# Two late sums of squares made in halves of 128 columns

## The chip, the core and the metric

The kernel runs on one core of a Trainium2 chip. It is one launch that computes two transformer blocks, one after the other, for 256 positions of width 1024 in float32. The metric is the device time of that launch in microseconds (us), given as the median of several executions.

## The reference, cut to what matters

The second block normalises its input four times. Two of these norms, before the feed-forward part and before the last gate, are the ones that the change touches:

```python
def rmsnorm(x, g):
    y = xf * lax.rsqrt(jnp.mean(xf * xf, axis=-1, keepdims=True) + EPS)
    ...
h = rmsnorm(x, g_ffn[i])                    # tag "nff"
u = jnp.einsum("bsd,df->bsf", h, w_up[i])   # 1024 -> 5632
...                                         # conv, gelu, product with w_down
pg = jax.nn.sigmoid(jnp.einsum("bsd,de->bse", rmsnorm(x, g_ple[i]), w_ple_gate[i]))  # tag "np"
```

A norm needs, for each of the 256 positions, the sum of the squares over the 1024 channels.

## The kernel before, in words

**Layout.** Channels lie on the 128 partitions and positions on the free axis: `xT[:, k, :]` is the k-th group of 128 channels, 256 positions wide (`T` = 256, `P` = 128, `NT` = 2, `KD` = 8).

**Products.** Each float32 weight matrix is loaded in chunks by SyncE. ScalarE writes a rounded copy `w_hi` of each chunk (`part`, L1175), VectorE the remainder `w_lo` (`rest`, L1743), and the activations are split in the same way into `h_hi` and `h_lo`. One block of 128 output channels is made of 24 matmuls of 256 columns, three for each k: hi by hi (L673), lo by hi (L674), hi by lo (L675); see `three`. `product_parted` does one block after another. `abreast` does the first four blocks of a stage together, with k outermost, since the activations come one k at a time. In the product with `w_down` the three matmuls stand on L1100, L1101 and L1102.

**The late norms.** The factor of a norm is one number for each position, so it is applied after the product and not before. ScalarE squares `xT` into `sq`, VectorE adds the eight groups up into two (`gather_squares`), and TensorE makes the sum over the partitions with a matrix of ones: `sum_two` (L1077 to L1082). It is called inside `abreast`, after k = 6 in the stage `up` and after k = 4 in the stage `pg`. The result lies in bank 2 of PSUM; nothing else uses that bank then. ScalarE takes the root of it (`late_root`, L1201, one instruction over all 256 positions, which waits for the semaphore `norm_ss`), VectorE the reciprocal (`inverse`, L2197), and only then VectorE takes the first products out of their banks (`scaled`, L2250).

**Order.** Each engine has its own written order of work; semaphores link them. TensorE goes through `up` (11 chunks of four blocks, 44 blocks), `down` (8 chunks, 528 matmuls), `pg` (2 chunks) and the final transposes and sums (L1114, L1135) without a break in its program. `begin` (L636) makes a block wait for the chunk's `w_lo` and for its bank to be emptied. VectorE handles one chunk of `up` in a fixed order: two products scaled, a convolution with three taps, two products by the gelu, then `rest` (L1743) for the next chunk but one. SyncE loads a chunk when the last product of the third chunk before it is done (L510).

Of the kernel before, what the change touches and what calls it, by code (L numbers as in the profile page):

```python
# [21 lines left out]
P = 128  # L22
T = 256
NT = T // P
# [187 lines left out]
def two_blocks(nc, w, out):  # L212
    with ExitStack() as ctx:
        made = {}

        def S(name):

            if name not in made:
                made[name] = ctx.enter_context(nc.semaphore(name))
            return made[name]  # L220

        def sb(name, shape, dt=F32):
            return ctx.enter_context(nc.sbuf_tensor(name, shape, dt))

        ps = ctx.enter_context(nc.psum_tensor("ps", [P, 8, 512], F32))
        BK = [ps[:, b, :] for b in range(8)]
# [8 lines left out]
        ident, ones = sb("ident", [P, P]), sb("ones", [P, P])  # L235
# [6 lines left out]
        sq = sb("sq", [P, KD, T])  # L242
# [183 lines left out]
        def f_lo(b):  # L426
            return f_lo2[b // 16][:, b % 16, :]
# [205 lines left out]
        def _(pe):  # L633
# [121 lines left out]
            for i in range(2):  # L755
                mm = pe.matmul(BK[i], ones[0:1, :], c_all[0:1, i * 512:(i + 1) * 512], start=True, stop=True)
# [29 lines left out]
            for b in range(2):  # L786
# [3 lines left out]
                if b == 0:  # L790
                    pe.wait_ge(S("taken_A"), taken_by("A", BLOCK_AT[("low", 0)]))
                    for t in range(NT):
                        mm = pe.transpose(BK[7][:, t * IH:(t + 1) * IH], low[32:32 + IH, t * P:(t + 1) * P],
                                          ident[32:32 + IH, 32:32 + IH])
# [11 lines left out]
            for h in range(GH):  # L806
                mm = pe.matmul(BK[4 + h // 2][:, (h % 2) * T:(h % 2 + 1) * T], wgate[0:16, h * P:(h + 1) * P],
                               low[0:16, :], start=True, stop=True)
            mm.then_inc(S("gate_mm"), 1)
            for b in range(4):  # L810
                plain("gq", b)
                if b == 0:
                    pe.wait_ge(S("kv_h"), 1)
                    for t in range(NT):
                        for i in range(2):
                            mm = pe.transpose(BK[7][:, t * LAT + i * P:t * LAT + (i + 1) * P],
                                              kvT[:, i, t * P:(t + 1) * P], ident[:, :])
# [10 lines left out]
            for i in range(2):  # L828
                for j in range(4 * i, 4 * i + 4):
                    mm = pe.transpose(BK[6 + i][:, (j % 4) * P:(j % 4 + 1) * P], ediff[:, j * P:(j + 1) * P], ident[:, :])  # L830
                mm.then_inc(S("kend_mm"), 1)
                plain("gr", i)
            for i in range(2):
                pe.wait_ge(S("kendT"), i + 1)
                for j in range(4 * i, 4 * i + 4):
                    h, t = j // 2, j % 2
                    mm = pe.matmul(BK[6 + i][:, (j % 4) * P:(j % 4 + 1) * P], gk[:, h, t * P:(t + 1) * P],
                                   gq[:, h, t * P:(t + 1) * P], start=True, stop=True)
# [3 lines left out]
            for n in range(3):  # L842
                t, half = n // 2, slice((n % 2) * CH, (n % 2 + 1) * CH)
                if n:
                    pe.wait_ge(S("state"), n)
                for h in range(GH):
                    mm = pe.matmul(BK[6 + h // 2][:, (h % 2) * DV:(h % 2 + 1) * DV], kendT[half, 2 * h + t, :],
                                   gv[half, t, h * DV:(h + 1) * DV], start=True, stop=True)
# [4 lines left out]
            for h in range(GH):  # L853
# [4 lines left out]
                for b in range(2):  # L858
                    for t in range(NT):
                        o = BK[6 + h % 2][:, b * T + t * P:b * T + (t + 1) * P]  # L860
                        mm = pe.matmul(o, gv[:, t, h * DV + b * P:h * DV + (b + 1) * P], attn[:, 2 * h + t, :],
                                       start=True, stop=False, skip_group_check=True)
                        for n in (2 * t, 2 * t + 1):
                            if n:
                                c = (n % 2) * CH
                                mm = pe.matmul(o[:, c:c + CH], state[:, n - 1, h, b * P:(b + 1) * P],
                                               gq[:, h, t * P + c:t * P + c + CH], start=False, stop=n % 2 == 1,
                                               skip_group_check=True)
# [45 lines left out]
            for h in range(AH):  # L914
# [5 lines left out]
                if h == 0:  # L920

                    pe.wait_ge(S("o_sq"), GH)
                    for i in range(GH):
                        for b in range(2):
                            mm = pe.matmul(BK[6 + i // 2][:, (i % 2) * T:(i % 2 + 1) * T], ones[:, :], gT[:, 2 * i + b, :],
                                           start=b == 0, stop=b == 1)
# [108 lines left out]
            for k in range(KD):  # L1035
                mm = pe.matmul(BK[3][:, 0:T], g2e[:, k:k + 1].broadcast_to([P, P]), sq[:, k, :],
                               start=k == 0, stop=k == KD - 1)
            mm.then_inc(S("nm_ss"), 1)
            for b in range(4, 28):
                product_parted(("z", b), h_hi, h_lo)  # L1040
                if b == 11:

                    pe.wait_ge(S("nm_added"), 1)
                    for k in range(2):
                        mm = pe.matmul(BK[2][:, T:2 * T], ones[:, :], sq[:, k, :], start=k == 0, stop=k == 1)
                    mm.then_inc(S("nm_ss"), 1)
                if b == 19:
# [4 lines left out]
                    for i in range(2):  # L1052
                        for n in range(PE_TAPS):
                            tap = CK - PE_TAPS + n
                            mm = pe.matmul(BK[2 + i][:, 0:T], tap_diag[:, i * PE_TAPS + n, :],  # L1055
                                           apad[:, 2 + i, tap:tap + T], start=n == 0, stop=n == PE_TAPS - 1)
# [20 lines left out]
            def sum_two(tag):  # L1077

                pe.wait_ge(S(tag + "_added"), 1)
                for k in range(2):  # L1080
                    mm = pe.matmul(BK[2][:, 0:T], ones[:, :], sq[:, k, :], start=k == 0, stop=k == 1)
                mm.then_inc(S("norm_ss"), 1)  # L1082

            abreast("up", 4, h_hi, h_lo, "up", between=lambda: sum_two("nff"))
            for b in range(4, 2 * FB):
                product_parted(("up", b), h_hi, h_lo)
            for j in range(4):
                outs = [begin(("down", 2 * j + b))[0] for b in range(2)]
                for half in range(2):
# [3 lines left out]
                    for b in range(2):  # L1093
                        o, cs = outs[b][:, 0:T], slice(b * P, (b + 1) * P)
                        for k in range(FB // 2):
                            f = half * FB // 2 + k
                            if j == 0 and b == 0:
# [4 lines left out]
                            mm = pe.matmul(o, hi[:, k, cs], f_lo(f), start=False, stop=f == FB - 1,  # L1102
                                           skip_group_check=True)
# [6 lines left out]
            def turn_out(k):  # L1110
# [5 lines left out]
                mm.then_inc(S("out_mm"), 1)  # L1116

            abreast("pg", 4, h_hi, h_lo, "pg", between=lambda: sum_two("np"), after=4)
            for b in range(4, 8):
                product_parted(("pg", b), h_hi, h_lo)  # L1120
# [9 lines left out]
            for k in (0, 5, 6, 7):  # L1130
# [3 lines left out]
                for t in range(NT):  # L1134
                    mm = pe.matmul(BK[4 + t][:, 0:1], sq[:, k, t * P:(t + 1) * P], ones[:, 0:1],  # L1135
                                   start=k == 0, stop=k == KD - 1, skip_group_check=True)
# [1411 lines left out]
```

## Time and profile before

| what | value |
|---|---|
| time, median of 3 executions | 1404.92 us |
| the three executions | 1404.68, 1404.92, 1409.11 us |
| the profiled execution: span from its first to its last instruction | 1410.0 us |
| its time around the span | not given apart from the span |
| TensorE matmul busy | 1242.9 us (88%) |
| VectorE busy | 1070.5 us (76%) |
| ScalarE busy | 618.2 us (44%) |
| mean granted clock of TensorE | 0.977 |

The profiled execution is one execution of its own: its span alone is 5.1 us longer than the median of the three timed ones. Times in the trace are counted from the start of that span. TensorE's matmuls are pipelined: one begins about 0.11 us after the one before, while its record lasts 0.28 us, so durations overlap and the distance of starts is what counts.

### The profile page before, as it was taken

What the parts mean: (1) busy time and instruction counts of PE and PEld (TensorE: products, weight loads), DVE (VectorE), ACT (ScalarE), POOL (GpSimd) and SP (SyncE); (2) the same over time, 40 slices, a digit from 0 to 9 for tenths busy, and PEclk for the clock granted to TensorE, in tenths of its full rate; (3) what the DMA queues carried; (4) which work ended last, traced back from release to release, by engine and by line L of the source; (5) the groups of instructions that cost most, each with busy time, mean ns of one, the idle gap of its engine ahead of it and who ended that gap; (6) DMA issues with size and microseconds to landing.
All of it is one profiled execution on the core that took longest, in us unless ns stands there. A gap on an engine that the chain in (4) does not pass through costs nothing. (4 is left out here: it accounts for less than half of the span.)

```text
span 1410.0 us, 19695 instructions
## 1 busy us (share of the span) xinstructions
PE 1242.9 (88%) x7042; PEld 933.2 (66%) x7042; DVE 1070.5 (76%) x2161; ACT 618.2 (44%) x1268; POOL 286.6 (20%) x278
## 2 busy tenths in 40 slices
PE   4999999999989877777877877878899999999998
PEld 3999999999944332332322323323599989999998
DVE  6898568587879777776777777776599968998556
ACT  4566465546344332333333332233563245544445
POOL 1000000000445444444444444443000000000000
PEclk8999999999999999999999999999899999999999
DMA  9946534554989999999999999999743344444461
GB/s 393 381 153 239 209 111 188 176 183 150 370 340 426 428 427 427 427 428 427 427 427 427 427 428 427 428 427 427 314 178 136 143 180 180 180 180 161 169 228 42
DMA packets 55808, 416.65 MB, mean 295 GB/s; under 512 B 6049, under 2 KB 7713, under 8 KB 9394
## 3 DMA queue, kind: packets, MB, share of 16 engines
q0 software_dynamic: 36864, 268.45, 45.3%
q1 hardware_dynamic: 18544, 146.78, 28.1%
q8 instruction: 51, 0.84, 0.2%
q10 hardware_dynamic: 322, 0.36, 0.1%
q14 instruction: 27, 0.22, 0.0%
HBM read 414.52 MB, written 1.05 MB: 295 GB/s over the span
## 5 line engine op out<-in xcount | busy, mean ns | idle before, releaser
L1015 PE MATMUL ps<-arena 128*128 128x512 f32 x512 | 239.4, 614 | 65.7 <-ACT arena L1478 65.7
L1015 PE MATMUL ps<-ring,arena 128*128 128x512 f32 x444 | 211.5, 628 | 46.3 <-ACT arena L1478 46.3
L1015 PEld LDWEIGHTS ps<-arena 128*128 128x128 f32 x512 | 94.6, 193 | 209.0 <-ACT arena L1478 107.0
L2093 DVE CUSTOM_DVE_ANT_0 arena<-arena 128x1024 f32<-128x1024 f32 x128 | 151.7, 1223 | 101.7 <-DMA arena<-in_experts,rowid 99.8
L597 POOL DMA_INDIRECT arena<-in_experts,rowid x128 | 131.7, 1029 | 379.2 <-DVE rowid L2070 208.2
L1015 PEld LDWEIGHTS ps<-ring,arena 128*128 128x128 f32 x444 | 86.2, 200 | 169.7 <-issue 93.2
L674 PE MATMUL ps<-h_hi,w_lo 128*128 128x256 f32 x704 | 198.0, 281 | 0.0
L673 PE MATMUL ps<-h_hi,w_hi 128*128 128x256 f32 x672 | 189.7, 282 | 0.7 <-DVE xT L2372 0.6
L1471 ACT ACTIVATE arena<-arena 128x2 f32<-128x2 f32 x126 | 25.6, 203 | 374.5 <-DVE arena L2093 374.4
L675 PE MATMUL ps<-h_lo,w_hi 128*128 128x256 f32 x672 | 187.9, 280 | 0.0
L1743 DVE TENSOR_TENSOR w_lo<-arena,w_hi 128x4096 fp32r<-128x4096 f32 (+1 forms) x31 | 126.5, 4080 | 39.8 <-ACT w_hi L1175 39.2
L597 POOL DMA_INDIRECT ring<-in_experts,rowid x112 | 128.3, 1146 | 137.8 <-PE ps L1015 93.6
L2093 DVE CUSTOM_DVE_ANT_0 ring<-ring,arena 128x1024 f32<-128x1024 f32 x112 | 133.3, 1222 | 29.7 <-DMA ring<-in_experts,rowid 20.5
L1175 ACT ACTIVATE w_hi<-arena 128x4096 fp32r<-128x4096 f32 (+1 forms) x31 | 103.9, 3351 | 74.8 <-DMA arena<-in_up_w 28.8
L674 PEld LDWEIGHTS ps<-h_hi,w_lo 128*128 128x128 f32 x704 | 134.1, 190 | 0.2
L1743 DVE TENSOR_TENSOR e_lo<-ring,e_hi 128x2048 fp32r<-128x2048 f32 (+1 forms) x48 | 109.0, 2275 | 26.3 <-ACT e_hi L1175 25.4
L673 PEld LDWEIGHTS ps<-h_hi,w_hi 128*128 128x128 f32 x672 | 128.1, 191 | 1.3 <-DVE w_lo L1743 0.8
L675 PEld LDWEIGHTS ps<-h_lo,w_hi 128*128 128x128 f32 x672 | 126.6, 188 | 0.0
L673 PE MATMUL ps<-n_hi,e_hi 128*128 128x256 f32 (+1 forms) x384 | 111.4, 290 | 4.0 <-DVE n_lo L1707 3.6
L674 PE MATMUL ps<-n_hi,e_lo 128*128 128x256 f32 (+1 forms) x384 | 106.8, 278 | 0.0
L675 PE MATMUL ps<-n_lo,e_hi 128*128 128x256 f32 (+1 forms) x384 | 106.8, 278 | 0.0
L1175 ACT ACTIVATE e_hi<-ring 128x2048 fp32r<-128x2048 f32 (+1 forms) x48 | 90.9, 1896 | 12.2 <-PE ps L675 9.4
(366 smaller groups left out, 2558.8 us busy)
## 6 DMA issues: line engine op xcount, KB each, us to landing
ring<-in_early_w SPq DMA_DIRECT2D x47, 1024.0 KB, 4.9
arena<-in_ada_w SPq DMA_DIRECT2D x24, 1024.0 KB, 7.4
arena<-in_up_w SPq DMA_DIRECT2D x11, 2048.0 KB, 7.7
arena<-in_z_w SPq DMA_DIRECT2D x8, 2048.0 KB, 7.8
arena<-in_down_w SPq DMA_DIRECT2D x8, 1408.0 KB, 5.9
arena<-in_o_w SPq DMA_DIRECT2D x2, 2048.0 KB, 8.0
arena<-in_pg_w SPq DMA_DIRECT2D x2, 2048.0 KB, 7.7
arena<-in_experts,rowid POOLq DMA_INDIRECT x128, 28.2
```

The source lines that it names most:

```text
L597: pool.indirect_dma_start(out=rows[j], out_offset=None, in_=w["experts"], in_offset=bass.IndirectOffsetOnAxis(ap=rowid[:, even, j:j + 1], ...
L673: pe.matmul(out, hi[:, k, c0:c0 + m], x_hi[:, k, :], start=k == 0, stop=False, skip_group_check=True)
L674: pe.matmul(out, lo[:, k, c0:c0 + m], x_hi[:, k, :], start=False, stop=False, skip_group_check=True)
L675: return pe.matmul(out, hi[:, k, c0:c0 + m], x_lo[:, k, :], start=False, stop=k == KD - 1, skip_group_check=True)
L1015: mm = pe.matmul(BK[4 + 2 * t + b], diag[:, j, :], rows[j][:, D + b * 512:D + (b + 1) * 512], start=first and j == 0, stop=last and j == ( ...
L1175: act.activation(hi, whole, ACT.Copy).then_inc(S("w_hi"), 1)
L1471: act.activation(gel[:, even, two], dots[:, even, two], ACT.Gelu).then_inc(S("act_head"), 1)
L1743: v.tensor_tensor(lo, whole, hi.bitcast(F32), ALU.subtract).then_inc(S("w_lo"), 1)
L2093: v.tensor_tensor_reduce(out=u, in0=u, in1=h2tok[:, t, :], scale=1.0, scalar=0.0, op0=ALU.mult, op1=ALU.add, accum_out=dots[:, even, j:j + ...
```

## The change

`sum_two` makes the sum in two halves of 128 positions. For each half it multiplies the two groups of squares by the matrix of ones, with the flag `start` on the first and `stop` on the second. Four matmuls of 128 columns take the place of two of 256 columns, in each of the two calls. Each of these float32 matmuls is run as two records (a weight load and a matmul each), so four records of 256 columns become eight of 128. The semaphore is still raised once, by the last one. The order of all other work, all tiles and all waits stay as they are.

```diff
             def sum_two(tag):
 
                 pe.wait_ge(S(tag + "_added"), 1)
-                for k in range(2):
-                    mm = pe.matmul(BK[2][:, 0:T], ones[:, :], sq[:, k, :], start=k == 0, stop=k == 1)
+                for t in range(NT):
+                    cs = slice(t * P, (t + 1) * P)
+                    for k in range(2):
+                        mm = pe.matmul(BK[2][:, cs], ones[:, :], sq[:, k, cs], start=k == 0, stop=k == 1)
                 mm.then_inc(S("norm_ss"), 1)
```

## Rows read from the trace of the kernel before

**Rows 1.** The profile page, head and first part: busy time by engine.
```profile
span 1410.0 us, 19695 instructions
PE 1242.9 (88%) x7042; PEld 933.2 (66%) x7042; DVE 1070.5 (76%) x2161; ACT 618.2 (44%) x1268; POOL 286.6 (20%) x278
```

**Rows 2.** The chain that ended last at both sums: start us, us, what.
```profile
1199.32 0.86 PE ps L1081 x4
...
1384.79 0.86 PE ps L1081 x4
```

**Rows 3.** The same chain from the down stage into the pg stage.
```profile
1361.33 7.55 DMA arena<-in_pg_w
...
1368.90 3.64 ACT w_hi L1175
...
1372.63 4.28 DVE w_lo L1743
...
1377.48 0.36 PE ps L673
```

**Rows 4.** Timeline of PE around the first sum: start us, us, engine, line, operation.
```profile
1189.97 0.28 PE L673 MATMUL ps<-h_hi,w_hi 128*128 128x256 f32 x1
...
1198.81 0.28 PE L673 MATMUL ps<-h_hi,w_hi 128*128 128x256 f32 x1
...
1199.15 1.02 PE L1081 MATMUL ps<-sq,ones 128*128 128x256 f32 x4
...
1200.13 0.28 PE L674 MATMUL ps<-h_hi,w_lo 128*128 128x256 f32 x1
```

**Rows 5.** Timeline of PE: eight float32 records of 128 columns between products.
```profile
140.00 1.06 PE L837 MATMUL ps<-arena 128*128 128x128 f32 x8
...
141.01 0.28 PE L674 MATMUL ps<-n_hi,e_lo 128*128 128x256 f32 x1
```

**Rows 6.** Busy time by engine, in 1202:1212 and in 1387:1397, with records touched.
```profile
1202.00:1212.00 10.00, 10.00 (x87) 10.00 (x86) 9.14 (x13) 6.93 (x6) 0.00 (x0) 1.00 0.58 212
...
1387.00:1397.00 10.00, 10.00 (x91) 10.00 (x90) 9.14 (x20) 6.07 (x16) 0.00 (x0) 1.00 0.00 0
```

**Rows 7.** Groups by line, 1190:1198, then 1202:1212: busy us, mean ns.
```profile
L674 PE MATMUL ps<-h_hi,w_lo 128*128 128x256 f32 x25 | 6.9, 276 | 0.0
...
L674 PE MATMUL ps<-h_hi,w_lo 128*128 128x256 f32 x29 | 8.1, 281 | 0.0
```

**Rows 8.** The same, 1040:1044.5, 1045.5:1050.5, 1052.2:1072 (a short wait, then L1045).
```profile
L674 PE MATMUL ps<-h_hi,w_lo 128*128 128x256 f32 x14 | 3.9, 276 | 0.0
...
L674 PE MATMUL ps<-h_hi,w_lo 128*128 128x256 f32 x15 | 4.2, 281 | 0.0
...
L674 PE MATMUL ps<-h_hi,w_lo 128*128 128x256 f32 x59 | 16.3, 276 | 0.0
```

**Rows 9.** The same, 137.6:139.6, 141.3:143.3, 145:147 (L837 twice between them).
```profile
L673 PE MATMUL ps<-n_hi,e_hi 128*128 128x256 f32 x6 | 1.7, 281 | 0.0
...
L675 PE MATMUL ps<-n_lo,e_hi 128*128 128x256 f32 x7 | 2.0, 281 | 0.0
...
L674 PE MATMUL ps<-n_hi,e_lo 128*128 128x256 f32 x7 | 2.0, 281 | 0.0
```

**Rows 10.** The same, 60.4:62.7, 63.6:65.9, 66.9:69.3 (L780, then L780 of 256 columns).
```profile
L674 PE MATMUL ps<-n_hi,e_lo 128*128 128x256 f32 x7 | 1.9, 276 | 0.0
...
L675 PE MATMUL ps<-n_lo,e_hi 128*128 128x256 f32 x7 | 1.9, 276 | 0.0
...
L674 PE MATMUL ps<-n_hi,e_lo 128*128 128x256 f32 x6 | 1.7, 281 | 0.0
```

**Rows 11.** Timeline of ACT, DVE and PE's weight loads from the first sum on.
```profile
1200.21 0.47 ACT L1201 ACTIVATE stat<-ps,epsc 128x256 f32<-128x256 f32 x1 [3.98 <-PE ps L1081]
...
1200.72 1.75 DVE L2197 RECIPROCAL stat<-stat 128x256 f32<-128x256 f32 x1
...
1208.10 4.42 DVE L1743 TENSOR_TENSOR w_lo<-arena,w_hi 128x4096 fp32r<-128x4096 f32 x1
...
1212.62 0.19 PEld L673 LDWEIGHTS ps<-h_hi,w_hi 128*128 128x128 f32 x1
```

## The prediction

> **What bounds the kernel now.** I began with the head of the page: TensorE's matmuls are busy 88% of the span, VectorE 76% [rows 1]. That is a mean over stages, so I went to the chain of waits at the two places of the change. Both sums stand on it with their full 0.86 us for four records [rows 2], and around them it consists of TensorE's product matmuls. In 1202:1212 TensorE is busy for all of 10.00 us [rows 6]. From the first sum to the end of `down` TensorE alone sets the pace. The chain leaves it once: the first chunk of `pg` waits for a load of 7.55 us, the rounding of 3.64 and the remainder of 4.28, and TensorE resumes at 1377.48 [rows 3]. So a TensorE nanosecond counts in full up to 1361.3 and again from 1377.5; between the two it hides.
>
> The third view is the one that matters most. The groups by line show that the same product matmul, same form, same granted clock of 1.00 (2.4 GHz) [rows 6], runs at two paces. Its record has a mean of 276 ns in 1190:1198 and of 281 ns in 1202:1212 [rows 7]. The distance of starts goes with it: from 1189.97 to 1198.81 are 78 matmuls, 8.84 / 78 = 0.1133 us each. From 1200.13 [rows 4] to the last matmul of the second `up` chunk, at 1212.62 beside the weight load of [rows 11], are 106 distances (the round k = 7 has 12 matmuls, four blocks have 96; counted from the second to the last), 12.49 / 106 = 0.1178 us. Counting records says the same: 87 touched in 10 us after the first sum and 91 after the second [rows 6]. The slow pace costs 0.0045 us a matmul, 3.8%, and it changes at the sums: fast before the first, slow after it for the whole of `up` and `down`, fast after the second.
>
> **The change part by part.** Removed: two times four records of 256 columns. From the start of the group at 1199.15 to the second product matmul at 1200.13 is 0.98; less one distance of 0.118, the group takes 0.862 [rows 4]. Added: two times eight records of 128 columns. The nearest row is L837, eight float32 records of that shape between products: 141.01 - 140.00 - 0.118 = 0.892 [rows 5]. The operands differ, not the shapes. Sum per call +0.03, for both +0.06 us. Bounds: the records could run at half of 0.215 each, 0.86, for no loss; or eight weight loads of 0.19 us [rows 11] and eight matmuls might not overlap at all, which rows 5 speak against (0.112 a record); that end is worked out as a rival.
>
> By the row, a record of 128 columns takes 0.112 us, more than half of 0.215. The Trainium skill, page "TensorE: Matmul & The Clock Gate", section "LDWEIGHTS (loading the stationary operand)", puts a load at its columns over 1.2 GHz, 0.107 us here. An estimate by it: eight loads make a floor of 0.853 against 0.862 before, so the halves could not gain and would lose nothing; the sum would be -0.02 instead of +0.06 us.
>
> What waits for the sum moves with it. The root starts 0.2 us after the last record began, at 1200.21, and VectorE's reciprocal at 1200.72, right after it [rows 11]; both shift by 0.03. Queued behind the reciprocal are all of VectorE's steps for the chunk, up to the `w_lo` that ends at 1208.10 + 4.42 = 1212.52, and TensorE's weight load for that chunk stands at 1212.62 [rows 11]. So 0.03 us more just fits. No DMA, ScalarE or SyncE order is touched; 16 more TensorE instructions are issued while its queue is full of work.
>
> The pace after the sum. This is the term that could be large, and no row of before shows eight records of 128 columns entered at the fast pace. What the rows show of such groups: four of 256 columns flipped the pace each time (fast to slow at the first sum [rows 7], slow to fast at L1045 [rows 8], fast to slow at L780 [rows 10], slow to fast at the second sum [rows 6]). Four records of 128 columns entered fast left it fast [rows 10]. Eight of 128 entered slow left it slow, twice [rows 9]. Bounds for the first call: slow afterwards, as now, 0; or fast afterwards. Then TensorE would want its weights for the third chunk of `up` about 106 x 0.0045 = 0.48 us earlier, at 1212.2, but they are ready at 1212.55: the first 0.4 us are lost to a new wait, and a wait can flip the pace too (a short one between 1044.5 and 1045.5 turned fast into slow [rows 8]). If it stays fast, 1361.3 - 1212.7 = 148.6 us shrink by 3.8%, 5.6 us; what comes after 1361.3 is held by the load. For the single forecast I take 0: two groups of exactly this shape left the pace slow, and even where the fast pace is kept the new wait has to leave it so.
>
> For the second call the same rows say slow after slow. Today that stretch is fast: about 100 matmuls from 1385.9 on. Taking L837's row, it loses 100 x 0.0045 = 0.45 us; bounds 0 and 0.6.
>
> Sum: +0.06 + 0.45 = +0.5 us on the profiled execution, 1410.0 to 1410.5. The timed median was 1404.92, 5.1 below that span; carrying the difference over gives 1405.4 us.
>
> **The rivals.**
>
> *The fast pace is kept (faster).* For it: four records of 128 columns kept it [rows 10], and the change replaces exactly the group that flipped it. Against it: L837 [rows 9] and the new wait at 1212.5. Price: -5.6 + 0.06, at most 0.5 more in `pg`: 1399.4 us.
>
> *The timed executions already ran fast in `up` and `down`, and the new group leaves them slow (slower).* The timed median lies 5.1 us under the profiled span and one timed execution 4.4 us above the other two; 5.6 is what this stretch costs between the paces. If the pace at 1199 differs between executions (waits before it may set it), four records of 256 columns flip slow to fast in those, while eight of 128 leave slow slow. It decides from the first `up` chunk on, and costs 5.6 less the 0.4 of the wait, plus 0.06 and up to 0.45: about +5, 1410 us. Against it: the DMA-bound gather stage could account for the spread as well, and nothing in the trace shows a second execution.
>
> *Loads and matmuls of the halves don't overlap (slower).* 8 x (0.19 + 0.275) = 3.7 instead of 0.86, twice: +5.7, 1410.6 us. Rows 5 stand against it.
>
> *The change does nothing.* The pace ends as it does now after both calls; only +0.06 is left, 1405.0.
>
> **How the numbers follow.** The slow pace stays or the executions are the same mix as now (forecast, with the rival of no effect): 0.49. Fast pace kept: 0.34, and 0.01 for smaller gains from other mixes. Pace made slow: 0.15. No overlap: 0.01. About 0.3%, 4.2 us, is what a measurement of this kernel can tell from no change. So faster 0.35, same 0.49, slower 0.16. The range runs from the fast case, 1399, to the slow one, 1410; the forecast's own is 1404 to 1407.
>
> **What would show it.** L1083's groups: eight records per call and 0.89 us on the chain. The mean of L673 to L675 in the 10 us after the first sum: 281 ns and 87 records means that my forecast holds, 276 and 91 the faster rival, with a wait of TensorE for `w_lo` near 1212.5. In 1387:1397, 87 records instead of 91. The `down` stage ends at 1361.3 in the forecast, near 1355.7 in the rival. What would make me wrong is a pace after eight records entered fast that L837, entered slow, doesn't foretell.

## The result, and the profile after

| what | before | after |
|---|---|---|
| median of 20 executions each | 1405.57 us | 1410.43 us |
| lowest and highest | 1399.16, 1412.84 | 1405.53, 1415.94 |
| ratio, with its 95% interval | | 1.0029, 1.0016 to 1.0043 |
| profiled execution: span, own time | 1410.0, not given | 1408.8, 1410.58 us |

The time of an execution is its span plus 1.8 us. Measured in this way the change is slower by 0.3%. The same file timed twice more gave 0.9991 and 0.9995 (experiments 5 and 11), so this ratio isn't a property of the code alone. What follows shows a mechanism that fits all three; how much of the 0.3% it accounts for stays in part open.

The page of after, its head and first part:

```profile
span 1408.8 us, 19711 instructions
PE 1241.1 (88%) x7050; PEld 932.6 (66%) x7050; DVE 1070.5 (76%) x2161; ACT 618.4 (44%) x1268; POOL 286.4 (20%) x278
```

Eight more TensorE records; the other engines are unchanged [rows 1]. The chain of waits of after at the two sums (start us, us, what), which answers to [rows 2]:

```profile
1198.04 0.89 PE ps L1083 x8
...
1383.53 0.89 PE ps L1083 x8
```

So eight records of 128 columns take 0.89 us on the chain where four of 256 took 0.86. The chain into `pg` answers to [rows 3]; the load that ends `down`'s part of it begins at 1360.08 instead of 1361.33:

```profile
1360.08 7.76 DMA arena<-in_pg_w
...
1371.59 4.07 DVE w_lo L1745
...
1376.47 0.36 PE ps L673
```

The pace is read from the groups by line (busy us, mean ns), first in 1189:1197 ahead of the first sum, then in 1202:1212 behind it, then in 1376:1382 and 1386:1394 around the second sum. They answer to [rows 7]:

```profile
L674 PE MATMUL ps<-h_hi,w_lo 128*128 128x256 f32 x24 | 6.7, 281 | 0.0
...
L674 PE MATMUL ps<-h_hi,w_lo 128*128 128x256 f32 x29 | 8.1, 281 | 0.0
...
L674 PE MATMUL ps<-h_hi,w_lo 128*128 128x256 f32 x16 | 4.4, 276 | 0.0
...
L674 PE MATMUL ps<-h_hi,w_lo 128*128 128x256 f32 x25 | 6.9, 276 | 0.0
```

Before arrived at the first sum at the fast pace (276 ns) and left it at the slow one (281). After *arrived* slow and left slow; at the second sum it arrived fast and left fast, where before arrived slow. Whichever pace came in went out. From the first sum on both profiled executions are alike: before has 1410.0 - 1199.15 = 210.85 us behind the start of that group, after 1408.8 - 1197.88 = 210.92 (start of the group in the timeline of PE, below). The busy times in 1202:1212, in 1387:1397 and in 1220:1360 (us, then PE, PEld, DVE, ACT, POOL busy with records touched, granted clock, DMA share, GB/s) answer to [rows 6]: 87 records after the first sum as before, and 91 after the second, at a granted clock of 1.00, the 2.4 GHz level, in each.

```profile
1197.88 1.05 PE L1083 MATMUL ps<-sq,ones 128*128 128x128 f32 x8
```

```profile
1202.00:1212.00 10.00, 10.00 (x87) 10.00 (x87) 9.21 (x14) 6.92 (x6) 0.00 (x0) 1.00 0.47 191
...
1387.00:1397.00 10.00, 10.00 (x91) 10.00 (x90) 9.28 (x23) 6.73 (x18) 0.00 (x0) 1.00 0.01 2
...
1220.00:1360.00 140.00, 140.00 (x1191) 140.00 (x1190) 106.44 (x142) 62.79 (x59) 0.00 (x0) 1.00 0.48 173
```

The last row is the ruler for all that follows: 1191 records in 140 us are 0.1176 us a matmul, and a kernel at the fast pace has 1238 there.

### The profile page after: what moved, and what is told of

It is laid out like the page before. It is cut to its first block and busy times, and to the rows that moved or that the text cites. A ratio compares the mean times of both kernels' runs of the same rounds, so it can differ in the third digit from the quotient of the medians.

```text
span 1408.8 us, 19711 instructions
## 1 busy us (share of the span) xinstructions
PE 1241.1 (88%) x7050; PEld 932.6 (66%) x7050; DVE 1070.5 (76%) x2161; ACT 618.4 (44%) x1268; POOL 286.4 (20%) x278
## 5 line engine op out<-in xcount | busy, mean ns | idle before, releaser
L1015 PE MATMUL ps<-arena 128*128 128x512 f32 x512 | 235.6, 606 | 64.3 <-ACT arena L1480 64.3
L1015 PE MATMUL ps<-ring,arena 128*128 128x512 f32 x444 | 214.4, 634 | 46.5 <-ACT arena L1480 46.5
L1745 DVE TENSOR_TENSOR e_lo<-ring,e_hi 128x2048 fp32r<-128x2048 f32 (+1 forms) x48 | 109.0, 2276 | 25.4 <-ACT e_hi L1177 24.5
```

Of the source, the lines that this page charges most:

```text
L1015: mm = pe.matmul(BK[4 + 2 * t + b], diag[:, j, :], rows[j][:, D + b * 512:D + (b + 1) * 512], start=first and j == 0, stop=last and j == ( ...
L1745: v.tensor_tensor(lo, whole, hi.bitcast(F32), ALU.subtract).then_inc(S("w_lo"), 1)
```

## The experiments

**1 and 2. One sum in halves at a time.** In experiment 1 only the first sum (tag `nff`) is made in halves, in experiment 2 only the second (`np`).

```diff
+                if tag == "nff":
+                    for t in range(NT): ...   # halves, as in the change
+                else:
+                    for k in range(2): ...    # as before
```

> Only the first late sum (before the feed-forward part) is made in halves; the second stays at 256 columns. Pace theory: four records of 256 columns turn the product pace over, eight of 128 leave it as they found it, so in the executions that come to the first sum at the slow pace the kernel before runs up and down fast and this one slow. It then carries nearly the whole loss of the change: ratio to before 1.002 to 1.004, about +4 to +5 us, product matmuls at 281 ns in the 10 us after the sum wherever they have 281 ns before it. Rival, direct cost: the halves cost only their own 0.03 us and the delay of the root, so the ratio is 1.000, or the loss is shared between the two calls (+2.5 us each).

> Only the second late sum (before the last gate) is made in halves. Pace theory: what can turn there is the pace of about 100 matmuls, 0.45 us at most, so ratio 1.000 within 0.0015. Rival, direct cost shared by both calls: +2.5 us, ratio 1.0017. Rival, eight more TensorE instructions shift the fetching of code: the same loss as with the first call alone.

Measured: first only 1404.31 us median of 12, ratio 0.9995 (0.9972 to 1.0019); second only 1405.48, ratio 1.0002 (0.9984 to 1.0019). So neither half of the change repeats the 0.3%. The profile of experiment 1 is 9.0 us shorter than that of after (span 1399.8): 5.1 of them lie behind the start of the first sum, and 3.9 ahead of it, where the two programs are the same. Its PE timeline has the group, and the group rows for 1196:1204, behind it, and the waits of PE in 1200:1215 (what waited, for what, us, times, longest) follow:

```profile
1193.97 1.05 PE L1084 MATMUL ps<-sq,ones 128*128 128x128 f32 x8
```

```profile
L674 PE MATMUL ps<-h_hi,w_lo 128*128 128x256 f32 x24 | 6.6, 276 | 0.0
```

```profile
PE ps L673 <- DVE w_lo L1749: 0.2, 1, 0.2
```

Eight records of 128 entered fast left the pace fast. Behind the group lie 1399.8 - 1193.97 = 205.8 us against 210.9 in after. My expectation had the first sum carry the loss; it missed, because what the group does depends on the pace that comes in. In experiment 2 the first sum is the old one: it turned fast into slow, and the second, in halves, kept slow (281 ns on both sides). Behind the start of the second sum lie 1406.6 - 1380.76 = 25.8 us there, and 1410.0 - 1384.62 = 25.4 in before, which left it fast.

**3 and 4. Many groups of one form in one execution.** After every second block of `up` from the sixth on, a useless sum goes to a bank that isn't in use: twenty groups of four records of 256 columns in experiment 3, of eight of 128 in experiment 4. The sums of the norms stay as before.

```diff
+            def probe():
+                for k in range(2):
+                    pe.matmul(BK[3][:, 0:T], ones[:, :], sq[:, k, :], start=k == 0, stop=k == 1)
             for b in range(4, 2 * FB):
                 product_parted(("up", b), h_hi, h_lo)
+                if b % 2:
+                    probe()
```

> The kernel before with a group of four float32 records of 256 columns, of no use, into bank 3 after every second block of the up stage, 20 groups with 48 product matmuls between them. Pace theory: the pace turns over at each group, so that records of 276 and 281 ns alternate from stretch to stretch, about ten of each. Rival: the pace depends on the stage or on what VectorE and ScalarE do, then it does not follow the groups. Own cost 20 x 0.86 = 17 us; half the stretches fast gives back up to 2.

> The same with eight records of 128 columns in each of the 20 groups. Pace theory: the pace after the original sum stays the same over all 20 groups unless TensorE waits for VectorE in between, all 281 ns or all 276. Rival, the shape does not matter: it alternates as with 256 columns. Own cost 20 x 0.89 = 18 us.

One execution each: 1420.35 and 1419.65 us. The group rows of experiment 3 in 1194:1199.4, 1201:1205.8, 1207.5:1212.3 and 1213.9:1218.6, with one useless group between each two:

```profile
L674 PE MATMUL ps<-h_hi,w_lo 128*128 128x256 f32 x16 | 4.5, 281 | 0.0
...
L674 PE MATMUL ps<-h_hi,w_lo 128*128 128x256 f32 x15 | 4.1, 276 | 0.0
...
L674 PE MATMUL ps<-h_hi,w_lo 128*128 128x256 f32 x14 | 3.9, 281 | 0.0
...
L674 PE MATMUL ps<-h_hi,w_lo 128*128 128x256 f32 x15 | 4.1, 276 | 0.0
```

All twenty groups turned the pace over. In experiment 4 the execution arrived slow at the first sum, whose four records of 256 turned it to fast, and it stayed fast through all twenty groups of halves; the group row of 1201:1320:

```profile
L674 PE MATMUL ps<-h_hi,w_lo 128*128 128x256 f32 x301 | 83.1, 276 | 0.0
```

**5. The changed kernel again.**

> The changed kernel unaltered, timed again beside the kernel before. Its first profiled execution came to the first sum at the slow pace and left it slow; the kernel with only the first sum in halves came to it at the fast pace and lost nothing. Theory that chance in each execution sets the pace on arrival: the times of this kernel then spread over two heaps some 5 us apart (1400 to 1406 and 1408 to 1411), and the ratio to before may well come out nearer 1.000 than the 1.0029 of the first measurement. Rival, that the two halved calls together fix the arrival at slow: again about 1410 us, ratio 1.003, and a profile with 281 ns before and after the first sum.

Measured: 1403.22 us median of 12 (1400.37 to 1411.32) against 1407.69 of before, ratio 0.9991 (0.9966 to 1.0016). Here the seventeen executions of before fell into two heaps, seven in 1399.9 to 1402.9 and ten in 1407.5 to 1413.2, with nothing between. The other timings of before show no such empty middle. This profile arrived fast and stayed fast to the end of `down`. The chain there (start us, us, what), the PE timeline at the end of it, and the ruler:

```profile
1196.23 3.64 ACT w_hi L1177
...
1202.34 4.43 DVE w_lo L1745
```

```profile
1206.38 0.28 PE L675 MATMUL ps<-h_lo,w_hi 128*128 128x256 f32 x1
1206.82 0.38 PE L673 MATMUL ps<-h_hi,w_hi 128*128 128x256 f32 x1 [0.15 <-DVE w_lo L1745]
...
1207.16 0.28 PE L675 MATMUL ps<-h_lo,w_hi 128*128 128x256 f32 x1
```

```profile
1220.00:1360.00 140.00, 140.00 (x1238) 140.00 (x1237) 108.11 (x141) 64.52 (x63) 0.00 (x0) 1.00 0.52 190
```

Same code, same clock: 1238 matmuls in 140 us instead of 1191. A fast TensorE meets the new wait for `w_lo` that the prediction worked out: VectorE's 4.43 us end at 1206.77, and the three distances from 1206.38 to 1207.16 take 0.78 us instead of 0.34, so 0.44 is lost. The span is 1398.8, 10.0 us less than in the first profile of this same file; 5.5 of them lie behind the start of the first sum (210.9 against 205.4), and 4.5 ahead of it (1197.88 against 1193.36).

**6 and 7. Both forms in turn.** As in experiment 3, with the useless groups alternately four records of 256 columns and eight of 128 (experiment 6), or four of 256 and four of 128 (experiment 7), so that the groups of 128 meet both paces.

```diff
+            def probe(n):     # n counts the groups
+                if n % 2 == 0:
+                    for k in range(2): ...                      # 256 columns
+                else:
+                    for t in range(2):                          # experiment 7: range(1)
+                        for k in range(2): ...                  # 128 columns
```

> The kernel before with 20 groups of no use after every second block of the up stage, in turn four records of 256 columns and eight of 128. Theory (256 turns the pace over, 128 x 8 keeps it, from either pace): the stretches of 48 product matmuls between groups run slow, slow, fast, fast, slow, slow and so on, each group of 256 a change and each group of 8 x 128 none. Rival, that 8 x 128 keeps only the fast pace, as in the 20 of 20 cases seen there: after its first use at slow the sequence breaks.

> The same with four records of 128 columns (one half alone) in place of the eight. The only rows so far: four such records entered fast left it fast, and once entered slow left it fast. If four of 128 always leave the fast pace, the stretches after them all have 276 ns and the stretches after the groups of 256 all 281. If they keep what they find, the sequence is slow, slow, fast, fast as with eight.

Single executions of 1421.35 and 1420.49 us. The group rows of experiment 6 in 1196:1200.2, 1201.8:1206.5, 1208.2:1212.8, 1214.5:1219, 1221:1225.8 and 1227.5:1232; between them stand a group of 256, of 128, of 256, of 128, of 256:

```profile
L674 PE MATMUL ps<-h_hi,w_lo 128*128 128x256 f32 x13 | 3.7, 281 | 0.0
...
L674 PE MATMUL ps<-h_hi,w_lo 128*128 128x256 f32 x15 | 4.1, 276 | 0.0
...
L674 PE MATMUL ps<-h_hi,w_lo 128*128 128x256 f32 x15 | 4.1, 276 | 0.0
...
L674 PE MATMUL ps<-h_hi,w_lo 128*128 128x256 f32 x14 | 3.9, 281 | 0.0
...
L674 PE MATMUL ps<-h_hi,w_lo 128*128 128x256 f32 x15 | 4.2, 281 | 0.0
...
L674 PE MATMUL ps<-h_hi,w_lo 128*128 128x256 f32 x14 | 3.9, 276 | 0.0
```

Four records of 256 turn the pace over from either side; eight of 128 keep either; experiment 7 shows the same of four of 128. As far as these sums show, this is the whole effect of the change on the pace, and it has no sign of its own: it helps an execution that arrives fast and hurts one that arrives slow.

**8. Nine other groups.** Useless groups after the first 36 blocks behind the first four of `up`: a form under test in turn with the four records of 256 that turn the pace over, each form met twice.

```diff
+                forms = [(1, T), (1, P), (3, T), (4, T), (-1, P), (-2, P), (1, 64), (6, P), (1, 192)]
```

> The kernel before with a group of no use after each of 36 blocks of the up stage: nine forms, each used twice and each time followed by four records of 256 columns, which turn the pace over, so that each form should be entered once at either pace (unless it changes the pace itself). The forms: one, three and four float32 matmuls of 256 columns; one and six of 128; one of 64; one of 192; one and two matmuls of 128 columns on rounded operands (a single record each). Theory A, every form either keeps the pace or turns it over, by how many columns it has: then no form can set it. Theory B, a few forms leave the same pace whatever they find: the one that always leaves 276 ns would take the chance out of the kernel.

It ran in 1438.02 us. Six records of 256 columns left the fast pace from either side, eight of 256 the slow pace from either side. A single matmul of 128 columns on rounded operands, or a single float32 one of 64, 128, 192 or 256 columns, always met the fast pace and left the slow one; two rounded ones and twelve float32 records of 128 kept either. The PE timeline with the six-record and the two eight-record groups, and then the group rows behind each (1240.6:1242.8, 1248.7:1251, 1257:1259.2):

```profile
1239.11 1.46 PE L1092 MATMUL ps<-sq,ones 128*128 128x256 f32 x6
...
1246.83 1.89 PE L1092 MATMUL ps<-sq,ones 128*128 128x256 f32 x8
...
1254.99 1.89 PE L1092 MATMUL ps<-sq,ones 128*128 128x256 f32 x8
```

```profile
L674 PE MATMUL ps<-h_hi,w_lo 128*128 128x256 f32 x7 | 1.9, 277 | 0.0
...
L674 PE MATMUL ps<-h_hi,w_lo 128*128 128x256 f32 x7 | 2.0, 281 | 0.0
...
L674 PE MATMUL ps<-h_hi,w_lo 128*128 128x256 f32 x7 | 2.0, 281 | 0.0
```

**9, 10 and 11. Groups that set the pace, and the changed kernel a third time.** If six records set the fast pace and eight the slow one, the times of whole executions should follow. One (experiment 9) or two (experiment 10) useless matmuls go ahead of both sums, into bank 3 and not, as my expectation has it, into the bank of the result:

```diff
+                for i in range(1):   # experiment 10: range(2), stop=i == 1
+                    pe.matmul(BK[3][:, 0:T], ones[:, :], sq[:, i % 2, :], start=i == 0, stop=i == 0)
                 for k in range(2):
                     mm = pe.matmul(BK[2][:, 0:T], ones[:, :], sq[:, k, :], start=k == 0, stop=k == 1)
```

> The kernel before, and in each of the two sums one useless matmul of 256 columns into the bank of the result ahead of the two: six records of TensorE instead of four. Pace theory: six records leave the fast pace whichever they meet, so up and down run at 0.1133 us a matmul in every execution; the profile shows the fast pace (276 ns) from the first sum to 1361, and the same stretch takes 6.1 us less than at the slow one. Own cost two times 0.43 us. Median 1400 to 1403, ratio to before 0.996 to 0.999, and few executions above 1406. Rival, that the pace is by chance of the execution and not set by the sum: the times are spread as before (1399 to 1413), and the ratio is 1.0005.

> The same with two useless matmuls of 256 columns ahead of the two in each sum: eight records. Pace theory: they leave the slow pace whichever they meet, so up and down run at 0.1178 us a matmul; the profile shows 281 ns from the first sum to 1361. Time 6.1 + 0.9 us above the six-record kernel: 1407 to 1411, ratio to before 1.001 to 1.004. Rival (pace by chance, only the useless work counts): 0.86 us above the six-record kernel, ratio to before 1.001.

> The changed kernel a third time, on the same chip as the six- and the eight-record kernel. Pace theory: both sums keep the pace that they meet, so its executions lie in two groups, near the six-record kernel less 0.8 us and near the eight-record kernel less 1.7 us, and so do those of before, with the groups' shares changed about; the ratio may come out on either side of 1 (0.998 to 1.003). Rival, that the halves are slower by themselves: ratio 1.002 to 1.004 as in its first timing, against 0.9991 in its second.

| | median | lowest, highest | above 1406.1 us | ratio (95%) |
|---|---|---|---|---|
| before | 1408.42 | 1400.36, 1416.85 | 17 of 29 | |
| six records | 1408.09 | 1400.20, 1413.65 | 7 of 12 | 1.0017 (0.9990 to 1.0044) |
| eight records | 1410.40 | 1406.44, 1419.74 | 12 of 12 | 1.0023 (1.0000 to 1.0046) |
| changed kernel | 1407.79 | 1399.20, 1410.45 | 7 of 12 | 0.9995 (0.9969 to 1.0020) |

Counted above 1407 us, as elsewhere here, before has 16 of 29, and the six records still 7 of 12. Eight records did as expected: no execution lies at the lower times. Their own extra work is 1.7 us by the 0.215 us a record; without it the lowest would be 1404.7, against 1400.36 in before. Six records did not do as expected: their times are spread as those of before, which is what the rival said. But their profile is as the theory has it: slow before the sum (1185:1191), fast behind it (1196:1204) and to the end of `down`. The two group rows, then the ruler for six records and for eight:

```profile
L674 PE MATMUL ps<-h_hi,w_lo 128*128 128x256 f32 x18 | 5.1, 281 | 0.0
...
L674 PE MATMUL ps<-h_hi,w_lo 128*128 128x256 f32 x24 | 6.6, 276 | 0.0
```

```profile
1220.00:1360.00 140.00, 140.00 (x1237) 140.00 (x1237) 107.69 (x140) 65.42 (x63) 0.00 (x0) 1.00 0.52 190
```

```profile
1220.00:1360.00 140.00, 140.00 (x1191) 140.00 (x1190) 105.76 (x142) 61.53 (x59) 0.00 (x0) 1.00 0.48 175
```

Yet seven timed executions took over 1407 us. In the profile only one interruption of TensorE's stream lies behind the first sum and ahead of the end of `down`, and only where the pace is fast: the wait for `w_lo`. In its PE timeline it stands at 1206.31:

```profile
1206.31 0.39 PE L673 MATMUL ps<-h_hi,w_hi 128*128 128x256 f32 x1 [0.15 <-DVE w_lo L1745]
```

At the slow pace there is no such wait, which may be why eight records held. Can a wait of this kind turn the pace? It did once in a profile, and elsewhere it did not. In experiment 10, ahead of the first sum, TensorE waits for `w_lo` at 1173.45. The group row of 1163.5:1173, the wait in the timeline of PE, and the group row of 1174:1179.5:

```profile
L674 PE MATMUL ps<-c_hi,w_lo 128*128 128x256 f32 x29 | 8.0, 276 | 0.0
...
1173.45 0.39 PE L673 MATMUL ps<-c_hi,w_hi 128*128 128x256 f32 x1 [0.18 <-DVE w_lo L1745]
...
L674 PE MATMUL ps<-c_hi,w_lo 128*128 128x256 f32 x15 | 4.2, 281 | 0.0
```

Fast went in and slow came out. The other five short waits for `w_lo` that a fast TensorE met between 1165 and 1215 in the profiles (at 1207.44, 1206.82 and 1206.31 in experiments 1, 5 and 9, at 1171.17 and 1174.34 in 6 and 7) left it fast. So such a wait can turn the pace, but one in six is fewer than the seven in twelve that experiment 9 would need. The third timing of the changed kernel came out level with before, as expected of the mechanism; its profile arrived slow and stayed slow (1191 in the ruler).

**12. Six records behind that wait.** The sums are as before; one useless group of six records follows the tenth block of `up`.

```diff
             for b in range(4, 2 * FB):
                 product_parted(("up", b), h_hi, h_lo)
+                if b == 9:
+                    for i in range(3):
+                        pe.matmul(BK[3][:, 0:T], ones[:, :], sq[:, i % 2, :], start=i == 0, stop=i == 2)
```

> The kernel before with both sums as they were, and one useless group of three matmuls of 256 columns (six records) after the tenth block of up, near 1212, behind the place where TensorE can wait for w_lo (1206 in fast profiles). It costs about 1.29 us. Six records at the first sum left the fast pace in both profiles, but 7 of 12 timed executions were above 1407. Theory A, that six records set the fast pace and the short wait at 1206 turned it afterwards in those: here nothing turns it afterwards, every execution does up and down from 1212 to 1362 at the fast pace, its time is that of its first sum (1192 to 1199 over the profiles) plus 206.5 to 209, so 1400 to 1409, with none above 1410. Theory B, that six records do not fix the pace: the times are spread as before plus 1.3 us, with some third of them above 1410. Profile: 276 ns from 1214 to 1362 by A.

Measured: 1403.39 us median of 12, all in 1401.40 to 1406.01, against 1405.20 (1400.06 to 1411.75, 8 of 17 above 1407), ratio 0.9982 (0.9964 to 1.0000). The profile turned from slow (1205:1211) to fast (1218:1228) at the group, and has 1238 in the ruler. The group in the PE timeline, and then the two group rows:

```profile
1216.00 1.46 PE L1089 MATMUL ps<-sq,ones 128*128 128x256 f32 x6
```

```profile
L674 PE MATMUL ps<-h_hi,w_lo 128*128 128x256 f32 x18 | 5.1, 281 | 0.0
...
L674 PE MATMUL ps<-h_hi,w_lo 128*128 128x256 f32 x31 | 8.6, 276 | 0.0
```

With 1.29 us of useless work in it (six times 0.215), this kernel has a lower median than before timed beside it, and none of its executions lies above 1407. Theory A held, though its range had been given wider, up to 1409. The 4.6 us that are left between its executions fit the start of the first sum, which lies between 1191.9 and 1199.4 over the profiles. It is the best version of the study by its ratio; the interval reaches to no change.

## Why the prediction was right and where it was wrong

The forecast was 1405.4 us and no change; measured were 1410.43, just outside the range of 1399 to 1410, and a ratio of 1.0029. The forecast change was +0.5 us, the medians differ by 4.9, and the interval (1.0016 to 1.0043) lies wholly above 1. In so far as "no change" held, in the two later timings, it held by luck: the term that I took as 0 is about -5.5 us against before in an execution that arrives fast and +5.5 in one that arrives slow, and over a mix of arrivals these can cancel. Point by point:

- *The sum's own cost, +0.03 us a call.* Right: 0.89 against 0.86 on the chain. The estimate that stood beside it, from the Trainium skill's page "TensorE: Matmul & The Clock Gate" (section "LDWEIGHTS (loading the stationary operand)"), was a floor of 0.853 for eight loads; this case's 0.89 lies above it and decides. One reading beside it was off: the root at 1200.21 starts 0.4 us after the last record began and not 0.2 (three distances of 0.215 behind 1199.15 are 1199.80); the sum doesn't use it.
- *A pace that costs 0.0045 us a matmul, 5.6 us over `up` and `down`.* Right in size. Behind the start of the first sum lie 210.9 us in after and 1398.8 - 1193.36 = 205.4 in experiment 5's profile of the same kernel; that is 5.5, with the wait of 0.44 paid.
- *Four records of 256 turn the pace over.* Right: twenty of twenty in experiment 3.
- *Eight of 128 entered fast: "for the single forecast I take 0", that is slow afterwards.* This step failed. They leave it fast (experiments 1, 5 and 6). The two groups at L837 that I rested it on [rows 9] had been entered slow and so couldn't tell "leaves it slow" from "keeps it"; the nearer row was that of four records of 128, which kept the fast pace [rows 10].
- *The second call: slow after slow, +0.45 us.* Wrong in after, which arrived fast and left fast, and right for experiment 2, which arrived slow: it depends on the arrival. There the price was right too, 25.8 us behind the start of that sum against 25.4.
- *A new wait for `w_lo` of 0.4 us where the pace is fast.* Right: 0.44, at the first block of the third chunk, 13.4 us behind the start of the group (1206.8 - 1193.4), where I had put it 13.3 behind (1212.5 - 1199.2).
- *"A wait can flip the pace too."* Right. Experiment 10 shows it for a short wait for `w_lo`. All 14 profiles show it at another, the last wait ahead of the first sum (0.55 to 0.75 us, for VectorE's addition to `xT`): of twelve that entered it fast, eight left it fast and four slow, and of two that entered it slow, one left it fast. Lines of it stand below the list. Experiments 9 and 12, which differ in the place of the six records, in front of the wait at 1206 or behind it, have 7 of 12 and none of 12 above 1407; but they ran on different chips (12 and 13).
- *The tail's bound by the load of `pg`.* As read: after's chain passes through it again.
- *The rivals.* "The timed executions already ran fast, and the new group leaves them slow", 1410 us with a chance of 0.15, is what the first measurement looks like: 17 of the 20 executions of after lay above 1408, and its profile kept slow what arrived slow. But "the fast pace is kept", 1399.4, is just as true of the same code: experiment 5's profile had 1398.8, and seven of twelve executions lay below 1404. They were never rivals about the code, but two cases of one mechanism, told apart by the pace at which an execution arrives. Both kernels are a mix over executions, and by this mechanism the change exchanges which arrivals end up at which pace. 47 of 107 timed executions of before were above 1407 us, and 27 of 44 of the changed kernel (17 of 20, then 3 and 7 of 12). If before turns the pace over where the changed kernel keeps it, the two shares of one timing should add up to 1; they are 0.25 and 0.85, then 0.59 and 0.25, then 0.55 and 0.58. That fits, but these are times: a start of the first sum that varies from 1191.9 to 1199.4 us moves a time by more than the pace does, so a time near 1407 doesn't tell the pace for certain.

The wait for `xT` in experiment 9: the group row of 1171.3:1176.6, and then the wait in the timeline of PE. Behind it the mean is 281 ns up to the sum (the row of 1185:1191 above):

```profile
L674 PE MATMUL ps<-c_hi,w_lo 128*128 128x256 f32 x14 | 3.9, 276 | 0.0
...
1176.82 0.36 PE L673 MATMUL ps<-c_hi,w_hi 128*128 128x256 f32 x1 [0.74 <-DVE xT L2374]
```

The rule "128 keeps, 256 turns over" is that of these sums and does not hold for every group of that size. Four records of transposes of 128 columns (L1116) stand between products of `pg`. In after they were entered fast and left slow, with no idle time shown before them; the group row of 1393:1396, the group, and the row of 1397.4:1399.6:

```profile
L674 PE MATMUL ps<-h_hi,w_lo 128*128 128x256 f32 x10 | 2.8, 276 | 0.0
...
1396.52 0.60 PE L1116 MATMUL ps<-ident,arena 128*128 128x128 f32 x4
...
L674 PE MATMUL ps<-h_hi,w_lo 128*128 128x256 f32 x7 | 2.0, 281 | 0.0
```

In experiment 11, the same file, the same group at 1394.45 was entered fast and left fast. So the form of a group and the pace at its entry don't decide alone.

Not settled: what sets the pace of arrival. No edit touched anything ahead of the first sum, and yet five of the fourteen profiles arrived slow (after and experiments 4, 8, 9 and 11) and nine fast. The wait for `xT` is where the paces of the profiles part, but its length doesn't tell which way: 0.73 us went before slow (experiment 4) and before fast (experiment 3). Why 17 of the first 20 timed executions of after had the longer times, and those of experiments 5 and 11 not, is open with it. The chips differed too (13, 10 and 12 in experiments 1, 5 and 11), and no run separates the chip from chance. That the wait at 1206 turned the pace in the upper times of experiment 9 is not shown: it rests on times and on experiment 12, and the three profiles that met it there passed it fast. That six records don't always leave the fast pace is the other reading; five groups of five speak against it, and no timed execution shows which. Why TensorE has two paces at all isn't shown by anything here.

## What to carry to other kernels

When one group's mean duration takes two close values (276 and 281 ns here) at one granted clock, count matmuls in a long stretch of several executions before pricing a change against one profile; a change of a few records can then show 0.3% either way with nothing gained or lost. If times fall into two heaps, look for what turns the pace over, and try a cheap group that fixes it behind the last short wait ahead of the long stretch; here that gave 0.9982, with an interval that reaches 1. Evidence on a state must include the entry state: a group that was only seen entered slow says nothing of it entered fast.

## What the runs showed of the hardware that I had not expected

At a granted clock of 1.00 the same stream of 256-column matmuls runs at 0.1131 us (1238 in 140 us) or at 0.1176 us (1191), and holds the one or the other for 1400 matmuls on end. Short insertions act on it by their form: four float32 records of 256 columns turn it over (22 of 22 in experiments 3 and 4 with the first sums), four, eight or twelve of 128 kept it where they made such a sum (four transposes of 128 did not always), six of 256 left it fast in five groups of five, eight of 256 left it slow in four groups of four with experiment 10's two sums. Waits act on it without a form: one of 0.73 to 0.74 us turned fast into slow in four of the twelve profiles that entered it fast, and one of 0.55 us turned slow into fast in experiment 10.
